# The lowest four doubling levels of a triangular inverse, moved from TensorE to VectorE by way of memory, and the first block resequenced

## The reference, cut to what matters

```python
proj = n @ w_in
aq, ak, av, az, aa, ab, bq, bk, bv, iq, ik, iw = jnp.split(proj, SPLIT_POINTS, axis=-1)
o_a = gated_deltanet(aq, ak, av, az, aa, ab, conv_a, a_log, dt_bias, a_out_norm)
o_b = dsa_attention(bq, bk, bv, iq, ik, iw, q_norm, k_norm, kidx_norm, cos_a, sin_a, cos_i, sin_i)
gates = jax.nn.sigmoid(n @ w_gate + b_gate).reshape(Bsz, T, 2, D)
y = gates[:, :, 0] * (o_a @ w_branch_a) + gates[:, :, 1] * (o_b @ w_branch_b)
return y @ w_out
```

```python
m = jnp.where(strict, bc[..., None] * kk * decay, 0.0)
lhs = m + jnp.eye(CHUNK, dtype=f32)
sol = lax.linalg.triangular_solve(lhs, rhs, left_side=True, lower=True, unit_diagonal=True)
```

## Time and profile before

| | |
|---|---|
| median of 3 runs | 1647.28 us (1644.95 to 1648.62) |
| the profiled execution | 1648.24 us |
| its span, first to last instruction | 1646.5 us |
| mean granted TensorE clock | 0.997 |
| PE busy | 1618.3 us, 98% |
| DVE busy | 1184.2 us, 72% |
| ACT busy | 922.5 us, 56% |
| transfers | 257.04 MB, 156 GB/s on average |

### The profile page before, as it was taken

How to read it: one execution, slowest core, us unless ns; L and a number is a source line. 1 busy time by engine, 2 the same in 40 slices (tenths; PEclk the granted TensorE clock), 3 DMA queues, 4 the chain that set the end, 5 groups by cost and what they waited for, 6 DMA issues and landing times.

```text
span 1646.5 us, 36115 instructions
## 1 busy us (share of the span) xinstructions
PE 1618.3 (98%) x13193; PEld 1577.5 (96%) x13193; DVE 1184.2 (72%) x1936; ACT 922.5 (56%) x1457; POOL 66.6 (4%) x58
## 2 busy tenths in 40 slices
PE   8999999999999999999999999999999999999998
PEld 7999989999999999899999989999999999999998
DVE  7879768766569688587765668888756846678763
ACT  5765464655446664656554555666545445566642
POOL 2002001000010020000000000000000000000000
PEclk9999999999999999999999999999999999999999
DMA  6542135555554430265666653565665544546663
GB/s 201 162 134 71 54 107 181 172 167 179 171 172 139 141 114 12 82 192 175 211 192 187 191 167 116 155 204 179 191 187 184 160 147 140 181 144 200 185 186 114
DMA packets 258862, 257.04 MB, mean 156 GB/s; under 512 B 13081, under 2 KB 257445, under 8 KB 258771
## 3 DMA queue, kind: packets, MB, share of 16 engines
q1 hardware_dynamic: 257523, 252.57, 49.5%
q0 software_dynamic: 1056, 3.08, 0.7%
q10 hardware_dynamic: 192, 0.14, 0.0%
HBM read 254.71 MB, written 1.05 MB: 155 GB/s over the span
## 4 chain that ended last, share of the span: by engine, by line
PE 86%; DVE 7%; ACT 3%; issue 2%; DMA 1%; DVEq 0%; ACTq 0%; SPq 0%
PE lin L525 22%; PE lin L528 22%; PE lin L533 22%; PE aux L834 8%; PE lin L834 3%; PE lin L579 3%; DVE wL L512 2%; PE lin L610 1%; PE lin L550 1%; DVE nT L2442 1%; DMA stage<-in_w_branch_b 1%; PE aux L1011 1%; DVE nL L2447 1%; DVE score L2179 1%; PE aux L533 0%
## 5 line engine op out<-in xcount | busy, mean ns | idle before, releaser
L503 ACT ACTIVATE wH<-stage 128x1024 fp32r<-128x1024 f32 (+1 forms) x488 | 492.9, 1049 | 454.7 <-PE lin L528 340.1
L512 DVE TENSOR_TENSOR wL<-stage,wH 128x1024 fp32r<-128x1024 f32 (+1 forms) x488 | 572.4, 1215 | 136.7 <-PE lin L533 75.5
L525 PE MATMUL lin<-nH,wH 128*128 128x256 f32 (+2 forms) x2256 | 559.0, 286 | 2.0 <-DVE u L2491 1.6
L528 PE MATMUL lin<-nL,wH 128*128 128x256 f32 (+2 forms) x2256 | 554.3, 285 | 0.0
L525 PEld LDWEIGHTS lin<-nH,wH 128*128 128x128 f32 x2256 | 425.1, 188 | 4.9 <-issue 2.9
L528 PEld LDWEIGHTS lin<-nL,wH 128*128 128x128 f32 x2256 | 426.2, 189 | 1.0 <-issue 0.7
L533 PE MATMUL lin<-nH,wL 128*128 128x256 f32 (+2 forms) x2256 | 295.0, 283 | 0.0
L533 PEld LDWEIGHTS lin<-nH,wL 128*128 128x128 f32 x2256 | 281.4, 188 | 0.3 <-DVE wL L512 0.3
L525 PE MATMUL lin<-aH,wH 128*128 128x256 f32 (+1 forms) x704 | 172.3, 284 | 0.0
L528 PE MATMUL lin<-aL,wH 128*128 128x256 f32 (+1 forms) x704 | 172.2, 284 | 0.0
L525 PEld LDWEIGHTS lin<-aH,wH 128*128 128x128 f32 x704 | 132.8, 189 | 0.0
(11 more groups left out here) (408 smaller groups left out, 2331.0 us busy)
## 6 DMA issues: line engine op xcount, KB each, us to landing
stage<-in_w_up SPq DMA_DIRECT2D x88, 512.0 KB, 4.6
stage<-in_ffn_w_up SPq DMA_DIRECT2D x88, 512.0 KB, 4.1
stage<-in_w_in SPq DMA_DIRECT2D x52, 512.0 KB, 4.8
stage<-in_w_down SPq DMA_DIRECT2D x40, 512.0 KB, 3.6
stage<-in_ffn_w_down SPq DMA_DIRECT2D x40, 512.0 KB, 4.1
stage<-in_w_gate SPq DMA_DIRECT2D x32, 512.0 KB, 3.9
stage<-in_even_w_in SPq DMA_DIRECT2D x24, 512.0 KB, 4.7
stage<-in_w_out SPq DMA_DIRECT2D x16, 512.0 KB, 4.4
```

The costliest lines, as they stand in the source:

```text
L503: nc.scalar.activation(wH[:, s, ks, 0:n], stage[:, s, ks, 0:n], ACT.Copy).then_inc(sem["whi"], 1)
L512: nc.vector.tensor_tensor(wL[:, s, ks, 0:n], stage[:, s, ks, 0:n], wH[:, s, ks, 0:n].bitcast(F32), ALU.subtract).then_inc(sem["wlo"], 1)
L525: mm = nc.tensor.matmul(banks[b][0:rows_, 0:width], wH[:, s, k, cols], xh, start=start and n == 0, stop=False)
L528: mm = nc.tensor.matmul(banks[b][0:rows_, 0:width], wH[:, s, k, cols], xl, start=False, stop=False)
```

## The change

The doubling levels 0 to 3 work inside the 16 x 16 squares on the diagonal of M. Of these there are 68: 8 squares by 4 heads in each 128-token block, and 4 for the 16 tokens. They now leave TensorE:

- SP writes `MT` of each block to scratch memory (`um`), when DVE has made it, and reads the diagonal squares back into `U`, one system to a partition, in rows of 16 numbers.
- DVE (`solved`) inverts all 68 at once. For n = 2, 4 and 8 it multiplies, sums over the last axis, multiplies and sums again, with 4, 2 and 1 instructions in each of the four steps, and one instruction ahead and one behind.
- SP writes the results `B` and the transposed `Bt` into zeroed scratch (`za`, `zx`), waits for these, and reads them as whole blocks into `A` and `X`.
- PE does the levels 4, 5 and 6 on the two 128-token blocks alone (`below`, `joined`). Level 4 needs no transposes.

The panel of the index queries moves ahead of z, the numbers of the panels shift (3 index queries, 4 z, 5 index and attention keys, 6 queries), and index products and scores come ahead of the norms of the queries. The gates' products stand between the levels. `kt` and `vt` move behind the first product of level 4. The orders of ACT, DVE and PE through the mixer of the first block are rewritten for both layers, and `JOBS` with them. POOL zeroes the scratch once. The diff, cut to its core:

```diff
-LEVELS = 7
+UPPER = (4, 5, 6)
+SYSTEMS = 4 * (2 * (P // META) + 1)
...
-    + [x for b in range(3) for x in (f"kt{b}", f"vt{b}")] + ["Y0_0", "Y1_0", "Y2_0"]
-    + [f"sbq{h}" for h in range(4)] + ["sbk", "sik"]
     + [f"ix0{e}" for e in range(2)] + [f"ix1{e}" for e in range(4)]
-    + [("loop", LEVELS - 2, ["Y0", "Y1", "T1", "Y2", "T2", "XA0", "X1", "X2"])] + ["Y1_6", "T1_6", "Y2_6", "T2_6", "s0", "A1", "A2"]
-    + ["vn0"] + [f"s{h}1" for h in "abcd"] + ["o0", "dS0", "pt0", "kS1", "pv0"] + [f"pt{b}_1" for b in range(2)] + ["vn1"]
+    + [f"sbq{h}" for h in range(4)] + ["sbk"] + ["Y1_4", "Y2_4"] + [x for b in range(3) for x in (f"kt{b}", f"vt{b}")]
+    + ["X1_4", "X2_4", "Y1_5", "T1_5", "Y2_5", "T2_5", "X1_5", "X2_5", "Y1_6", "T1_6", "Y2_6", "T2_6", "vn0", "s0"]
+    + ["o0", "dS0", "A1", "A2"] + [f"s{h}1" for h in "abcd"] + ["kS1", "pt0", "vn1", "pv0"] + [f"pt{b}_1" for b in range(2)]
...
+        um = [nc.dram_tensor(f"um{b}", (4, TB[b][1] + 1, TB[b][1]), F32) for b in range(3)]
+        za = [nc.dram_tensor(f"za{b}", (4, TB[b][1] + 1, TB[b][1]), F32) for b in range(3)]
+        zx = [None] + [nc.dram_tensor(f"zx{b}", (4, P + 1, P), F32) for b in (1, 2)]
...
+        def diagonal(t, b):
+
+            n = TB[b][1]
+            return bass.AP(t, 0, [[META * n + META, 4 * (n // META)], [n, META], [1, META]])
...
+                gate(0, 0)
+                for b in range(3):
+                    kept_off(b)
+                sp.wait_ge(sem["mt_out"], at("mt_out", l, 48))
+                for b in range(3):
+                    sp.dma_start(systems(U, b), diagonal(um[b], b)).then_inc(sem["mt_in"], 16)
+                gate(0, 1)
+                if l == 0:
+                    sp.wait_ge(sem["scratch"], 4 * 16)
+                sp.wait_ge(sem["solved"], at("solved", l, 1))
+                for b in range(3):
+                    sp.dma_start(diagonal(za[b], b), systems(B, b)).then_inc(sem["inverse_out"], 16)
+                for b in (1, 2):
+                    sp.dma_start(diagonal(zx[b], b), systems(Bt, b)).then_inc(sem["inverse_out"], 16)
+                sp.wait_ge(sem["inverse_out"], at("inverse_out", l, 80))
+                for b in (1, 2):
+                    sp.dma_start(X[b], by_token(zx[b], b)).then_inc(sem["inverse_in"], 16)
+                for b in (1, 2, 0):
+                    sp.dma_start(A[b], by_token(za[b], b)).then_inc(sem["inverse_in"], 16)
+                with sp.Fori(1, 4) as i:
...
-                w_in(5, 0)
+                w_in(6, 0)
                 keys_and_queries(0)
                 keys_and_queries(1)
-                w_in(5, 1)
                 decays(2)
+                w_in(6, 1)
                 keys_and_queries(2)
-                w_in(6, 0)
...
+                def below(level):
+
+                    for b in (1, 2):
+                        if level > UPPER[0]:
+                            pe.wait_ge(*read(f"X{b}_{level - 1}", l))
+                        else:
+                            pe.wait_ge(sem["inverse_in"], at("inverse_in", l, 80))
+                        pe.wait_ge(sem["ml"], at("ml", l, 2 * (level - UPPER[0]) + b))
+                        ps = begin(f"Y{b}_{level}", l)
+                        for h in range(4):
+                            t = mm(ps[:, h * P:(h + 1) * P], ML[b][:, h, :], X[b][:, h, :])
+                        t.then_inc(filled(f"Y{b}_{level}"), 1)
...
+                index_products(0)
+                gate(0, [0])
+                index_products(1)
+                pe.wait_ge(sem["sq_att"], at("sq_att", l, 1))
+                for h, name in enumerate([f"sbq{h}" for h in range(4)] + ["sbk"]):
+                    mm(begin(name, l)[:, 0:T], ones, sq_att[:, h, :]).then_inc(filled(name), 1)
+                gate(0, [1])
+                below(4)
...
+                joined(4)
                 gate(1, [0])
...
+                below(5)
+                gate(1, [1])
+                joined(5)
...
+                gate(2, [0])
+                below(6)
                 new_values(0)
+                scores(0)
+                gate(2, [1])
+                delta_out(0)
+                joined(6)
                 scores(1)
-                gate(2, [0])
-                delta_out(0)
+                state_seen(1)
                 weights_turned(0)
-                gate(2, [1])
-                state_seen(1)
+                gate(3, [0])
+                new_values(1)
...
+                index_relu(0)
+                gate_hi(0, [0])
+                index_relu(1)
+                root_log([f"sbq{h}" for h in range(4)] + ["sbk"], rnb, 1.0 / P)
+                root("sbk", rnb, 0.0)
+                gate_hi(0, [1])
+                below(4)
+                for b in range(3):
+                    n = TB[b][1]
+                    act.wait_ge(*full(f"vt{b}", l))
+                    f(vt[0:n, b], bank(f"vt{b}")[0:n, :].rearrange("p (h d) -> p h d", h=4), Copy).then_inc(emptied(f"vt{b}"), 1)
+                gate_hi(1, [0])
+                below(5)
+                gate(0)
+                gate_hi(1, [1])
+                below(6)
...
+                def solved():
+
+                    dve.wait_ge(sem["mt_in"], at("mt_in", l, 48))
+                    u, x = (t.rearrange("p j c -> p (j c)")[:, 1:META * META:2 * META + 2] for t in (U, B))
+                    own.done(v.tensor_scalar(x, u, -1.0, None, ALU.mult))
+                    for n in (2, 4, 8):
+                        starts = range(0, META, 2 * n)
+
+                        def products(left, right):
+                            own.wait()
+                            for q, r in enumerate(starts):
+                                to = prod[:, q * n ** 3:(q + 1) * n ** 3].rearrange("p (j c i) -> p j c i", j=n, c=n)
+                                own.done(v.tensor_tensor(to, bf(left(r), 2, [SYSTEMS, n, n, n]), bf(right(q, r).rearrange("p i c -> p c i"), 1, [SYSTEMS, n, n, n]), ALU.mult))
+
+                        def sums(to, negate):
+                            own.wait()
+                            for q, r in enumerate(starts):
+                                own.done(v.tensor_reduce(to(q, r), prod[:, q * n ** 3:(q + 1) * n ** 3].rearrange("p (j c i) -> p j c i", j=n, c=n), AX, ALU.add, negate=negate))
+
+                        def partial(q, r):
+                            return part[:, q * n * n:(q + 1) * n * n].rearrange("p (i c) -> p i c", i=n)
+
+                        products(lambda r: U[:, r:r + n, r + n:r + 2 * n], lambda q, r: B[:, r + n:r + 2 * n, r + n:r + 2 * n])
+                        sums(partial, False)
+                        products(lambda r: B[:, r:r + n, r:r + n], partial)
+                        sums(lambda q, r: B[:, r:r + n, r + n:r + 2 * n], True)
                     own.wait()
-                    masked(b, 1)
-                split_lo(dve, m0 + M_GATE, 1)
-
-                def added(n, x, turned):
-
-                    dve.wait_ge(sem["rope_cos"], at("rope_cos", l, n + 1))
-                    dve.wait_ge(sem["rope_sin"], at("rope_sin", l, n + 1))
-                    v.tensor_tensor(x, x, turned, ALU.add).then_inc(sem["rope"], 1)
-
-                def times_sin(n, x):
-
-                    dve.wait_ge(sem["swapped"], at("swapped", l, n + 2))
-                    table = const("sin_i", T)[:, T - x.shape[2]:T]
-                    v.tensor_tensor(x, x, bf(table, 1, list(x.shape)), ALU.mult).then_inc(sem["rope_sin"], 1)
-
-                def crossed(to, x):
-
-                    for p0, p1 in ((0, 64), (64, 0)):
-                        table = const("sin_a", T)[p1:p1 + 64]
-                        ins = v.tensor_tensor(to[p0:p0 + 64], x[p1:p1 + 64], bf(table, 1, [64, x.shape[1], T]), ALU.mult)
-                    ins.then_inc(sem["rope_sin"], 1)
-
-                queries, keys = rawT[:, 16:20, :], bkr[:, :].unsqueeze(1)
-                dve.wait_ge(sem["rn"], at("rn", l, 3))
-                v.scalar_tensor_tensor(ikr[:, :], ikr[:, :], pc(K_IN), rni[:, 0, :], ALU.mult, ALU.mult).then_inc(sem["att_unit"], 1)
-                dve.wait_ge(sem["rn"], at("rn", l, 4))
-                v.scalar_tensor_tensor(bkr[:, :], bkr[:, :], pc(K_KN), rnb[:, 4, :], ALU.mult, ALU.mult).then_inc(sem["att_unit"], 1)
-                v.scalar_tensor_tensor(rawT[:, 16:20, :], rawT[:, 16:20, :], pc(K_QN), rnb[:, 0:4, :], ALU.mult, ALU.mult).then_inc(sem["att_unit"], 1)
-                times_sin(0, iq_s[:, :, :])
-                times_sin(1, ik_s[:, :].unsqueeze(1))
-                gate_lo(0, [0])
-                added(0, rawT[:, 20:24, META:T], iq_s[:, :, :])
-                added(1, ikr[:, :].unsqueeze(1), ik_s[:, :].unsqueeze(1))
-                split_lo(dve, m0 + M_GATE + 1, 0)
-                dve.wait_ge(sem["att_unit"], at("att_unit", l, 3))
-                crossed(bk_s[:, :].unsqueeze(1), keys)
-                crossed(tmp4[:, :, :], queries)
-                gate_lo(0, [1])
-                added(2, keys, bk_s[:, :].unsqueeze(1))
```

(101 more changed lines are left out.)

378 lines of the change are left out of this document (159 added, 219 removed).

## The result

The changed kernel takes **1693.49 us**, the median of 4 runs (1692.85 to 1694.05); the kernel before had 1647.87 in the same comparison. The ratio is 1.028, with a 95% interval of 1.0262 to 1.0298. The forecast was 1694 us, slower, and the range 1656 to 1718 held it.

A forecast was written before the change was run, and what follows sets the result against it. PE, 98% busy, bounds the kernel. Per layer, stall 28.5 plus other waits 15.7 less saving 22.3 is +21.9; two layers +43.8 and clock +3.4 on 1648.24 give 1695.4, median 1694 us; range 1656 to 1718.

The forecast's parts named there:

- The bound: Whole kernel: PE, busy 98% of the span, sets the time; DVE, ACT and transfers count only through PE.
- The saving: PE's inverse: loop 29.7 and transposes 1.2 go, 3.85 and 4.7 return for levels 4 and 5; 22.3 us a layer.
- The chain: From product kk2 to PE's squares of the queries: round trip, loads, splits and solve in one line, 39.4 us.
- The stall: PE idle ahead of the squares of the queries: 39.4 less 10.95 of work beside it, 28.5 us a layer.
- The other waits: PE waits before the decays, at kS1 and from gate(3,0) on: together 15.7 us a layer, bounds 0 and 22.
- kS1: State product for block 1, waiting for a bank that DVE's greatest(1) reads: 7.5 us a layer.
- In front of the decays: ACT and DVE swap halves for keys and queries and split z's panels in a new order: 4.5 us a layer.
- Behind gate(3,0): Low half 0.6 late, and a head's scores wait 3.1 for vn1, read by ACT: 3.7 us a layer.
- The clock: PE at 1.2 GHz after four long stalls: 6.8 us, less layer 1's old idle time and its loss, +3.4.
- rival 1: Memory round trip exposed ahead of the squares, no further waits show: +15.8 us, 1663 us; chance 0.16.
- The second: Rival on the scratch transfers: 64 B pieces are dear, 9.7 us more a layer, 1714 us; chance 0.12.
- The third: Rival on the memory round trip: covered by PE's work, so the kernel gets faster, 1599 us; chance 0.08.

The follow-up runs named there:

- the last two moves: Each against the changed kernel: kS1 and its bank put ahead of block 1's scores, 1697.55 us; DVE's last four rounds and bias put before the inverse, 1681.79 us.
- the wide rows: Changed kernel with the four big writes of solved squares as 1 KB rows in place of 64 B pieces, output not the reference's: 1691.59 us.
- the two moved loads: Changed kernel with gate(1,0) loaded ahead of the wait for the solve and gate(0,1) ahead of the writes of MT: 1644.11 us.
- the first load moved: Changed kernel with only the first slot of w_gate's second panel, gate(1,0), loaded ahead of SP's wait for the solve: 1665.56 us.

## Why the prediction was right, step by step

**The bound.** That PE's time alone decides held in every run: PE's busy time differs little between the kernels from 1632 to 1706 us (1583.1 to 1593.9), its idle time makes the rest.

**The saving, 22.3 us a layer: somewhat too large.** PE is busy 28.7 us less and loses 11.4 more at the lower clock (14.8 − 3.4), so 40.1 were saved in two layers, against 44.6. The row for the loop had 29.70 us of time and 28.24 of work; I took the time. The 1.46 of idle in it isn't saved work, but a wait that goes away, and over two layers that is 2.9 of the 4.5; where the rest lies is open.

**The chain, 39.4 us: 40.4 measured.** Its terms in layer 0, forecast and then measured from the chain above: MT 0.6, 0.7; the write of um 3.5, 2.2; issues of U 1.2, 1.2; gate(0,1) 5.4, 5.1; ACT 3.7, 3.8; index scores 3.3, 3.4; solve 6.7, 7.5; the writes 4.3, 3.65; reads and gate(1,0) 9.2, 11.3; ACT 1.5, 1.6. The last big one was short: the reads' issues took 0.4 to 0.6 each and not 0.373, and gate(1,0) was issued when X and A were still under way and landed 7 us later. The solve was short because each of its two products over 512 elements of 68 partitions takes 1.02 to 1.08 us, where I took 0.6 (the row for MT shows 0.69); its small operations took a little less than I gave them.

**The stall, 28.5 us a layer: 29.0 and 27.0.** It came in two pieces, one inside the index products (3.27 and 3.61), which I had counted to the cover. The sum is nearly the same.

**The other waits, 15.7 us a layer: some 5.5 too many in each.** This is the step that was mis-sized most. kS1 was right (7.5, measured 6.97 and 7.05), and its mechanism, DVE's work ahead of greatest(1), was shown by the last two moves; the bank alone was not the cause. In front of the decays 3.1 and 1.9 us came in place of 4.5. Behind gate(3,0), 0.6 and 1.9 net in place of 3.7. All idle times over 0.35 us grew by 74.8; the stalls are 56.1 of that, so all others, what before lost in its own places taken off, are 18.7 in place of 29.7 (2 × 15.7 less the 1.7 of before).

**The clock, +3.4 us with the hole of before: too small.** Without that hole it was 5.1, and 11.4 were lost. I charged 1.7 us a stall from one short idle time. The squares at 157 lose 2 us in 4, kS1 and what follows 2.6 of 5.15 busy us, and 210 to 212 loses 1 us with no long idle time close ahead of it. What brings that one about is open, so this step is only in part explained.

Together in us: the other waits 11.0 too many, the saving 4.5 too large, the clock 6.3 too small, the stalls 0.9 too long. The first and the last push the forecast up, the other two down: 11.0 + 0.9 − 4.5 − 6.3 leaves 1.1 too many. Another 1.6 is idle time of PE that went away outside these places and that I had no term for, 0.6 of it ahead of its first product. The profiled execution, 1692.85, is 2.5 under my 1695.4, and the median lies 0.6 above it, where I took 1.0 off. That the forecast stands 0.5 from the median is luck. The direction did not hang on it: with no other waits at all it would have been rival 1, 1663.

**The rivals.** The first had the stall right and the other waits at nothing; they are 18.7 us. The second fell with the wide rows. The third, a round trip that is covered, does not hold in the changed order, but its mechanism does: the two moved loads bring it about, all but 4 to 5 us a layer.

## What to carry to other kernels

Before a round trip through memory is put into a queue, look at what else that queue serves: here 49 of the 61 us that were won back came from two weight loads that stood in line behind it, not the trip. A wait shows at the first instruction that needs a late engine; moving that instruction only shows the second, and what helps is to look for the hole on the late engine just ahead of its burst. And count a stretch that goes away by its busy time, its idle time apart.

## What the runs showed of the hardware

- Short stalls can cost more clock than a long one. With the first load moved, PE's idle times fell by 30.9 us, but the time lost at the lower clock rose by 4.5, since more work fell into stretches at 0.50.
- The clock stood at 0.50 in a window in which PE was busy for the whole 2 us (210 to 212). Ahead of it stand products of the 16-token block, 16 x 16 and 16 x 128 in size, and no idle time over 0.25 us for nearly 50 us. Layer 1 of the same execution has no such stretch. The kernel before has one in layer 1, 4 us from 660 with PE busy throughout and the clock at 0.71 on average. What brings it about was not tried and stays open.
- 2,050 pieces of 64 B written to memory took 0.4 us more (3.65 and 3.21 from the first write to the first read) than the same bytes in rows of 1 KB, and a write of 256 KB landed in 2.2 us, sooner than I took from a load of that size, 3.5.
- On DVE a product whose operands are repeated and turned by their access patterns took 1.02 to 1.08 us for 512 elements on 68 partitions, a plain one of 128 partitions 0.69. That the patterns are the reason was not tried by a run.
